# Two transformer blocks on one core: inverse square roots moved to VectorE, the input also loaded turned, dummy products at the start, and an order of work counted in slots of six products

## What is computed

```
def rms_norm(x, g):
    y = x * rsqrt(mean(x * x, axis=-1) + 1e-6)
    return y * g

h = rms_norm(x, norm1_g)                       # stage X0
qa, ka, va, ra, ga, qb, kb, vb = split(h @ w_in)
out_a = gla_mixer(...)                         # ends in an rms_norm of each head
qb = rms_norm(qb, q_norm_g)                    # per head of 128 channels
kb = rms_norm(kb, k_norm_g)
out_b = dilated_mixer(qb, kb, vb, rel_bias)
x = x + concat(out_a, out_b) @ w_out
h2 = rms_norm(x, norm2_g)                      # stage X1
x = x + (silu(h2 @ w_gate) * (h2 @ w_up)) @ w_down
h = rms_norm(x, ev_norm_w)                     # stage X2
q, k, v, g_ret, gate_b, gate_c, u, g_conv = split(h @ ev_w_in)
ret = rms_norm_nogain(retention(rope(q), rope(k), v)) * silu(g_ret)
conv = gate_b * conv3(gate_c * u) * silu(g_conv)
x = x + concat(ret, conv) @ ev_w_out
h = rms_norm(x, od_norm_w)                     # stage X3
q, k, v, gate = split(h @ od_w_in)
q = rope(rms_norm(q, q_norm_w)); k = rope(rms_norm(k, k_norm_w))   # per head of 64
x = x + (swa_sinks(q, k, v, sinks) * silu(gate)) @ od_w_out
```

## Time and profile before

| | us |
|---|---|
| median of 3 runs (range) | 1968.02 (1967.99 to 1968.89) |
| the profiled execution | 1967.95 |
| its span in the profile | 1966.1 |
| TensorE busy | 1943.1 |
| VectorE busy | 1096.0 |
| ScalarE busy | 939.5 |
| GpSimd busy | 108.7 |

### The profile page before, as it was taken

The page is one execution under the profiler, slowest core; times in us unless marked ns, Lnnn a source line. Parts: engine busy times, 40 slices in busy tenths (PEclk is TensorE's granted clock), DMA queues, the critical chain, the costliest instruction groups (busy, mean ns, idle before and its releaser), DMA issues.

```text
span 1966.1 us, 22662 instructions
## 1 busy us (share of the span) xinstructions
PE 1943.1 (99%) x9046; PEld 1597.9 (81%) x9046; DVE 1096.0 (56%) x1330; ACT 939.5 (48%) x1230; POOL 108.7 (6%) x326
## 2 busy tenths in 40 slices
PE   8999999999999999999999999999999999999998
PEld 6788887788888888888888888888888888787787
DVE  4556465665445554455454556544655565666674
ACT  6545454554444344443444554444444364665653
POOL 1111000200000000000000010001100003001100
PEclk9999999999999999999999999999999999999999
DMA  7566554566665666665666566665566655544445
GB/s 234 181 190 174 154 175 156 163 181 183 194 191 191 193 193 187 189 191 192 194 191 190 182 192 186 192 194 170 164 188 186 192 182 172 151 150 140 137 150 162
DMA packets 182473, 352.77 MB, mean 179 GB/s; under 512 B 11152, under 2 KB 11968, under 8 KB 182368
## 3 DMA queue, kind: packets, MB, share of 16 engines
q1 hardware_dynamic: 181552, 349.22, 58.9%
q0 software_dynamic: 816, 2.11, 0.7%
HBM read 349.17 MB, written 2.11 MB: 179 GB/s over the span
## 4 chain that ended last, share of the span: by engine, by line
PE 93%; DVE 3%; POOL 1%; ACT 1%; issue 1%; DMA 0%; DVEq 0%; SPq 0%; ACTq 0%
PE g L796 29%; PE g L798 29%; PE g L797 29%; PE m L762 3%; DVE wl L1238 1%; ACT TW L995 1%; DVE st L1247 1%; PE m L877 1%; DVE TW L1238 1%; ACT wh L998 0%; POOL st L1606 0%; PE ob L894 0%; PE ob L895 0%; PE ob L893 0%; POOL st L1604 0%
## 5 line engine op out<-in xcount | busy, mean ns | idle before, releaser
L1238 DVE TENSOR_TENSOR wl<-raw,wh 128x1024 fp32r<-128x1024 f32 x656 | 801.1, 1224 | 769.3 <-ACT wh L998 768.7
L998 ACT ACTIVATE wh<-raw 128x1024 fp32r<-128x1024 f32 x657 | 694.6, 1058 | 835.6 <-PE g L798 832.8
L796 PE MATMUL g<-wh,xh 128*128 128x512 f32 x1888 | 748.3, 396 | 2.9 <-DVE wl L1238 2.9
L798 PE MATMUL g<-wh,xl 128*128 128x512 f32 x1888 | 736.8, 390 | 0.0
L797 PE MATMUL g<-wl,xh 128*128 128x512 f32 x1888 | 735.6, 390 | 0.0
L796 PEld LDWEIGHTS g<-wh,xh 128*128 128x128 f32 x1888 | 355.0, 188 | 80.1 <-issue 5.5
L798 PEld LDWEIGHTS g<-wh,xl 128*128 128x128 f32 x1888 | 354.6, 188 | 75.3
L797 PEld LDWEIGHTS g<-wl,xh 128*128 128x128 f32 x1888 | 355.2, 188 | 70.5
L796 PE MATMUL g<-wh,mh 128*128 128x512 f32 x736 | 291.5, 396 | 0.0
L798 PE MATMUL g<-wh,ml 128*128 128x512 f32 x736 | 287.1, 390 | 0.0
L797 PE MATMUL g<-wl,mh 128*128 128x512 f32 x736 | 286.7, 389 | 0.0
(11 more groups left out here) (130 smaller groups left out, 831.5 us busy)
## 6 DMA issues: line engine op xcount, KB each, us to landing
raw<-in_ev_w_in SPq DMA_DIRECT2D x128, 512.0 KB, 3.7
raw<-in_w_in SPq DMA_DIRECT2D x96, 512.0 KB, 3.9
raw<-in_w_gate SPq DMA_DIRECT2D x88, 512.0 KB, 4.4
raw<-in_w_up SPq DMA_DIRECT2D x88, 512.0 KB, 3.7
raw<-in_w_down SPq DMA_DIRECT2D x88, 512.0 KB, 4.6
raw<-in_od_w_in SPq DMA_DIRECT2D x72, 512.0 KB, 3.7
raw<-in_w_out SPq DMA_DIRECT2D x32, 512.0 KB, 4.7
raw<-in_ev_w_out SPq DMA_DIRECT2D x32, 512.0 KB, 4.6
```

The costliest lines, as they stand in the source:

```text
L796: e.matmul(o, hi[:, kt, c], h, start=first, stop=False)
L798: last = e.matmul(o, lo[:, kt, c], h, start=False, stop=end)
L998: return e.activation(o, i, AF.Copy, scale=scale)
L1238: return e.tensor_tensor(o, a, b, op)
```

## The change

**Roots.** `root` stands on VectorE, as twelve dependent operations on a tile of 128x2 to 128x16 (three-operand forms make the Newton step three operations long, or two in the last). GpSimd has no root left. In the plan a root is a step of its own ("qk_root", "g_root", "r_root", "on_root") behind the sum; so is the squaring ("qk_sq", "on_sq"). For a norm of x it stands directly behind the sum.

**Turned input.** The host gives x a second time as `xT`, channels first. Its 16 tiles are loaded in five parts into the tile A1, and a step "xsplit" makes `xh` and `xl` from SBUF, without TensorE. x itself is loaded later, in four parts beside units 6 to 9. The constants come later too, and the gains of the first norm (8 KB) through GpSimd's queue.

**Start.** The first unit is cut in two units of one tile (256 KB, six products), both loaded from ScalarE's queue. VectorE sets a part of a `wl` buffer to 0.5, and TensorE makes nine products of it into a bank that nobody reads ("warm").

**Plan.** A slot is a half unit, six products: `lay` makes a step of the lanes after each half. A chain says with `yield n` how many slots it pauses. Chains that ran one step in 12 products now have steps 1 to 4 slots apart. The transposes of a new x come before its squares.

```diff
+        starts = [0, 1] if b.i == 0 else []
+        starts += range(per if starts else 0, len(b.kts), per)
+        for a, z in zip(starts, starts[1:] + [len(b.kts)]):
+            units.append(Unit(len(units), b, b.kts[a:z], a == 0, z == len(b.kts)))
...
         for lane in self.lanes:
-            self.advance(lane)
+            self.pause[lane] -= 1
+            if self.pause[lane] <= 0:
+                self.advance(lane)
...
             say("mul", u, 0)
             self.step()
-            if b.n == 512:
+            if len(un.kts) == 2:
                 say("mul", u, 1)
+                self.step()
...
             say("qk_evac", key, j, b.i)
-            yield
-            say("qk_sum", key, j)
-            yield
-            yield
-            say("qk_norm", key, j)
-            yield
-            yield
+            for p in ("qk_sq", "qk_sum", "qk_root", "qk_norm"):
+                yield 1 if (b.i, p) == (0, "qk_sq") else 2
+                say(p, key, j)
+            yield 3 if b.i else 2
...
+            yield 1
             say("conv", j, 0)
-            yield
+            yield 2
             say("conv", j, 1)
...
     def od_norm(self, x):
-        self.say("on_sum", x)
-        yield
-        yield
-        self.say("on_norm", x)
-        yield
-        self.say("on_rope", x, 0)
-        yield
-        self.say("on_rope", x, 1)
+        for p in ("on_sq", "on_sum", "on_root", "on_norm"):
+            yield 2
+            self.say(p, x)
+        for k in range(2):
+            yield 1
+            self.say("on_rope", x, k)
...
     def retention(self):
         say = self.say
         for h in range(4):
             say("r_s", h)
-            yield
-            yield
+            yield 4
             say("r_pv", h)
-            yield
+            yield 2
             say("r_sum", h)
-            yield
-            yield
+            yield 1
+            say("r_root", h)
+            yield 2
             say("r_n", h)
-            yield
-            yield
+            yield 4
...
+                if kind == "warm":
+                    on.wait_ge(s_warm, 1)
+                    for i in range(9):
+                        last = e.matmul(MB[2][:, :], wl[:, 2, 0:128], wl[:, 2, 0:512], start=True, stop=True)
+                    last.then_inc(s_warmed, 1)
...
+            weights(e, 0).then_inc(s_raw[0], 16)
+            weights(e, 1).then_inc(s_raw[1], 16)
...
+            def root(dst, src, n, width, from_, dst_free=()):
+
+                v, y, q = rv_[:, 0:n], ry_[:, 0:n], rq_[:, 0:n]
+                yi = y.bitcast(i32)
+                on.wait_ge(*from_)
+                on.wait_ge(*steps.mark(e.tensor_scalar(v, src, 1.0 / width, 1e-6, ALU.mult, ALU.add)))
+                on.wait_ge(*steps.mark(ts1(yi, v.bitcast(i32), 1, ALU.logical_shift_right)))
+                on.wait_ge(*steps.mark(e.tensor_scalar(yi, yi, -1.0, 1597463007.0, ALU.mult, ALU.add)))
+                for i in range(3):
+                    on.wait_ge(*steps.mark(stt(q, v, -0.5, y, ALU.mult, ALU.mult)))
+                    on.wait_ge(*steps.mark(tt(q, q, y, ALU.mult)))
+                    if i < 2:
+                        on.wait_ge(*steps.mark(stt(y, q, 1.5, y, ALU.add, ALU.mult)))
+                for sem_n in dst_free:
+                    on.wait_ge(*sem_n)
+                stt(dst, q, 1.5, y, ALU.add, ALU.mult).then_inc(s_root, 1)
...
+                elif kind == "xsplit":
+                    kt = a[1]
+                    on.wait_ge(s_n1, 16)
+                    on.wait_ge(s_xt[[lo <= kt < hi for lo, hi in XPARTS].index(True)], 16)
+                    on.wait_ge(s_split, splits[p])
+                    for i in range(2):
+                        last = stt(xl[:, kt + i, :], xT[:, kt + i, :], C("n1", kt + i, kt + i + 1),
+                                   xh[:, kt + i, :].bitcast(f32), ALU.mult, ALU.subtract)
+                    last.then_inc(s_first, 1)
```

## The result

| | before | after |
|---|---|---|
| median of 6 runs each, us | 1968.01 | 1961.49 |
| range | 1967.70 to 1968.89 | 1960.36 to 1961.83 |
| the profiled execution / its span | 1967.95 / 1966.1 | 1960.36 / 1958.6 |
| forecast | | 1958.6 (1952.5 to 1965.0) |

The account below looks back on a forecast made before the run. The prediction took TensorE, busy 1943.1 of 1966.1 us, to bound the kernel. Start 6.0 plus waits 7.2, heads 0, less convolution 3.4 and small charges 0.4, gave 9.4 us: 1968.0 to 1958.6, range 1952.5 to 1965.0.

Parts of the forecast that it names:

- the forecast's own 1955.5 to 1962: Whole kernel: the band of times in which the forecast itself counts as met, given a 56% chance.
- Start: Program start: transposes removed (2.6), first product earlier (1.8) and high clock from it on (1.6) gain 6.0 us.
- The transposes of x: Program start: six groups of four transposes between products, 0.44 us each, leave TensorE and give 2.6 us.
- The clock: Program start: after nine dummy products the high clock holds from the first product on, giving 1.6 us.
- (b): Rival, start gives less: clock still low (1.6) and first transfers landing late (1.3), so 1961.5 us; 14%.
- Waits on roots: Query and key blocks: TensorE's waits on TW and wl and the slow restarts behind them go, gaining 7.2 us.
- Root: VectorE: twelve dependent steps of 0.21 us make a root 2.5 us, with bounds of 1.8 and 3.1.
- Convolution: Convolution: a root between its two halves delays a weight piece, a new TensorE wait costing 3.4 us (1.0 to 4.5).
- Heads: Last layer's gated heads: waits of 1.1 and 0.8 us replace 1.67 and 0.2, three times, so no gain.
- (c): Rival: the roots' waits only move, VectorE's roots holding up query and key pieces as GpSimd's did; 1965.8 us; 7%.
- (d): Rival, slower: dependent root steps cost far more than 0.21 us, 9.6 us lost per 0.1; loss from about 0.31; 5%.
- (a): Rival: VectorE runs freer than counted, so the convolution's wait and half of the heads' go; 1953 us; 18%.

Follow-up runs that it names:

- e1: Changed kernel with the first norm's gains (8 KB) issued at the head of SyncE's queue instead of GpSimd's; 1961.45 us.
- e2: Changed kernel with 18 dummy products at the start instead of nine; 1959.42 us.
- c2: Changed kernel with the third retention head's sum and root three slots later, behind the whole convolution; 1957.83 us, ratio 0.9949 to the kernel before.
- r1: Changed kernel with all 21 roots back on GpSimd at their new places, the shift staying on VectorE; 1974.14 us.
- b1: Kernel before with only its 21 roots moved to VectorE, directly behind their sums; 1980.95 us.
- d1: Changed kernel with seven Newton steps instead of three in every root, 24 dependent operations instead of 12; 1998.13 us.
- e4: Changed kernel with the first norm's gains early through SyncE's queue and 15 dummy products; 1959.42 us, ratio 0.9954 to the kernel before.
- c1: Changed kernel with four slots instead of two between the two halves of the convolution; 1958.75 us, ratio 0.9951 to the kernel before.

## Why the prediction was right, and where it wasn't

The time, 1961.5, lies within the forecast's own 1955.5 to 1962 and within the range. It does so because two errors of opposite sign met.

**Start: 6.0 forecast, 1.9 measured.** Three terms. The transposes of x, 2.6, went as worked out. The first product was to move from 8.77 to 7.0 and didn't: the step that failed took only the bytes of weights and turned x into account and left out the gains' 8 KB, which came last, at 6.7 us. The transfers of x were late as well: with the gains early, ScalarE still waited for the turned x until 5.54 (e1), for which I had 4.6 + 0.6. The clock was to give 1.6 and took 0.9 (slow products cost 2.8 us instead of 1.9). The step that failed compared the gap of "2 us" with that of the earlier trace rows. The gap was 3.65, because the first product was late. It also took for granted that nine dummies are enough. e1 tried the forecast's own case, nine dummies and a gap of 1.95: all nine stand 0.43 apart, the first seven products too, and the first record of the clock in the trace is at 10.5 us, so the high clock had not come and couldn't be lost in the gap. In e2, with eighteen and 1.49, no product was slow. In c2 and r1 the nine did bring it, and it fell behind gaps of 3.1 and 3.2 us. So either can fail; how much each is worth stays open, since no run varied one alone at a short gap. Rival (b), the start gives less, had both halves of this in kind, at 14%. That its 1961.5 is the measured median is luck: it has nothing of the 2.2 us gained elsewhere.

On the second half of rival (b) the Trainium skill (DMA: Bandwidth & Descriptors, "Issuing engines are not separate DMA queues") is not contradicted: the rate was 432 GB/s from 7 to 8 us and 389 from 9 to 14, where the earlier trace rows has 387 and 381 to 408, though two hardware queues were in use. The same page ("Latency and other measured facts") puts the first byte of a transfer from GpSimd at about 1 us against 0.6 from the hardware queues. Here 8 KB took 5.4 against 2.8 us to landing, a difference six times as large, with the other transfers in flight and another turn among them, so this is no measurement of the page's figure.

**Waits on roots: 7.2 forecast.** Right: 5.6 in the first stretch (5.4 in the working) and none on TW before 130 us. What it didn't see is to whom the gain belongs. In blocks 3 to 5 it is the new plan's alone, since r1 takes there what the changed kernel takes (22.7 us a block) and b1 more than the kernel before (24.2 against 23.65). In block 2 and in the last layer the new plan gains with VectorE's roots and loses with GpSimd's.

**Root: 2.5 forecast, 2.30 measured** (2.24 over 128x2). The estimate from the Trainium skill's fixed cost of an operation (VectorE: DVE Perf Modes, TRN2 errata), 0.17 a step, is the length of one step in the trace (0.16 to 0.18), but steps that wait for the one before them start 0.195 to 0.21 apart. The forecast's 0.03 for three-operand forms stands in no row; without it its own 0.19 a step gives 2.3, which is what was measured.

**Convolution: -3.4 forecast, -3.0 in the profile.** Right in place, size and mechanism. The step that is missing is the clock: 1.6 us more in five of six traces. With it the term is -4.6.

**Heads: 0 forecast.** The new waits of 1.1 and 0.8 a block are there, 0.93 and 0.65 above the usual spacing (TensorE stands 1.16 and 0.88 from a product to the transposes, where before it stood 2.06). Each is a little short of the forecast, which makes 0.3 of the 0.4 that each of the three pairs of blocks gained. The first query block gained 1.6, of the 1.8 that stood in the 7.2 for this layer.

**Rivals.** (c) fell by the first stretch. (d) did not happen, but its price was wrong: 36.6 us for 2.35 more a root is 18.7 us per 0.1 us a step, twice the 9.6 of the prediction. At that slope the gain of 6.5 is used up 0.035 us above the 0.20 of a step, not at 0.31 (for small additions the slope may be less; no run made one). What failed is the count of eight roots without cover, and the low clock behind the longer waits was not in the price. (a) is against the trace: VectorE was as busy at the convolution and the heads as counted.

## What to carry to other kernels

When serial work moves to an engine that feeds the bottleneck, cost it together with its place: the same roots cost 13 us in the old plan (b1), while in the new one GpSimd's cost 13 us more than VectorE's (r1). Count what stands between two pieces of the feeding engine, and put the chain where the lead has been rebuilt. Price an idle time of TensorE by the products behind it too. Warm-up products should reach up to the first real product, and the smallest input of that product should be issued ahead of the large ones.

## What the runs showed of the hardware

- **The clock can fall after an idle time in the middle of the program, and not at a fixed length of it.** Behind 1.67 us it stayed, three times (kernel before). It fell to 0.5 behind five waits of 2.0 to 2.6 (r1), five of six of 3.0 and three of 3.7 (b1), but behind only one of four of 2.3 to 2.4 in d1 (and behind its others, 2.2, 3.5, 3.7 and 5.3). For the waits of 3.0 that was 1.6 to 2.8 us of further loss.
- **When the clock rises at the start differs from run to run.** The dummies begin at 1.46 us in every trace with them; with nine or more, the high clock came at 4.3 us in the changed kernel, 4.9 in e2 and 7.5 in e4, and in e1 and c1 only behind the first products, at 10.5 and 13.5.
- **At a program's start the spacing of equal matmuls is the safer reading.** In e1 between 8 and 10 us the profile shows 1.00 and the products stand 0.43 apart: the trace has no record of the clock before 10.5 us, and the view shows 1.00 where there is none. In the kernel before the first record is at 12.6, just behind the last slow products.
- **GpSimd's small operations scatter**: 0.2 us mostly, 1.1 to 1.2 in one or two steps of each of seven roots looked at in r1, so the two roots of block 2 took 4.9 and 5.9 us against 2.3 on VectorE.
